# Expert gathers of a two-layer kernel: head 0 of tile 0 chosen alone, V rows eight behind U rows, query steps in thirds

## What is computed

```python
def peer(xn, w_pq, sub_k1, sub_k2, expert_u, expert_v):
    B, S, D = xn.shape
    q = (xn @ w_pq).reshape(B, S, PEER_HEADS, 2, PEER_HALF)
    s1 = jnp.einsum('bshd,hnd->bshn', q[..., 0, :], sub_k1, preferred_element_type=jnp.float32)
    s2 = jnp.einsum('bshd,hnd->bshn', q[..., 1, :], sub_k2, preferred_element_type=jnp.float32)
    v1, i1 = lax.top_k(s1, PEER_TOPK)
    v2, i2 = lax.top_k(s2, PEER_TOPK)
    cand = (v1[..., :, None] + v2[..., None, :]).reshape(B, S, PEER_HEADS, PEER_TOPK * PEER_TOPK)
    vs, ci = lax.top_k(cand, PEER_TOPK)
    e1 = jnp.take_along_axis(i1, ci // PEER_TOPK, axis=-1)
    e2 = jnp.take_along_axis(i2, ci % PEER_TOPK, axis=-1)
    eidx = e1 * PEER_NKEYS + e2
    gates = jax.nn.softmax(vs, axis=-1).astype(xn.dtype)
...
    def block(args):
        xb, ib, gb = args
        act = jax.nn.gelu(jnp.einsum('tkd,td->tk', expert_u[ib], xb))
        return jnp.einsum('tk,tkd->td', act * gb, expert_v[ib])
```

## Time and profile before

| | us |
|---|---|
| median of three runs | 2485.25 |
| profiled execution | 2483.89 |
| its span | 2482.5 |
| PE busy in the span | 2106.7 (85%) |
| VectorE busy | 1411.8 (57%) |
| ScalarE busy | 644.2 (26%) |
| POOL busy | 682.2 (27%) |
| bytes moved by DMA | 751.22 MB, 303 GB/s on average |

### The profile page before, as it was taken

One profiled execution on the slowest core, in us unless ns is written; L12 is line 12 of the kernel. 1 busy time (PEld: TensorE's weight loads), 2 busy tenths in 40 slices (PEclk: granted clock), 3 DMA queues, 4 the chain that ended last, 5 costly groups with the idle time before them and its releaser, 6 DMA issues.

```text
span 2482.5 us, 19393 instructions
## 1 busy us (share of the span) xinstructions
PE 2106.7 (85%) x7532; PEld 1345.7 (54%) x7532; DVE 1411.8 (57%) x1786; ACT 644.2 (26%) x884; POOL 682.2 (27%) x522
## 2 busy tenths in 40 slices
PE   8998948698887787777777777779999999999999
PEld 7876845254432332222222222226888778888887
DVE  4576686645568777454444444445554665654454
ACT  5454522111112010100000000004443353543342
POOL 0000045445455555444454545430000000000000
PEclk9999978999999999999999999989999999999999
DMA  7443469899999999999999999994455544455553
GB/s 274 157 153 104 168 272 398 358 421 397 372 422 421 421 421 422 421 422 421 421 422 422 421 422 422 422 404 160 183 189 194 177 161 170 170 191 195 191 179 143
DMA packets 105355, 751.22 MB, mean 303 GB/s; under 512 B 11952, under 2 KB 11952, under 8 KB 14384
## 3 DMA queue, kind: packets, MB, share of 16 engines
q0 software_dynamic: 73728, 536.90, 52.3%
q1 hardware_dynamic: 29376, 207.63, 23.4%
q10 hardware_dynamic: 2160, 5.45, 0.6%
HBM read 747.84 MB, written 2.10 MB: 302 GB/s over the span
## 4 chain that ended last, share of the span: by engine, by line
PE 51%; DMA 35%; DVE 9%; issue 2%; ACT 1%; POOL 1%; ACTq 0%; SPq 0%; DVEq 0%; POOLq 0%
PE ps L336 37%; DMA xT_rows<-in_expert_v,idx 23%; PE ps L647 10%; DMA wlo_row<-in_expert_v,idx 4%; DMA W<-in_expert_u,idx 2%; DMA xT_rows<-in_expert_u,idx 2%; DMA W<-in_expert_v,idx 2%; DVE wlo L1254 1%; DMA raw<-in_expert_u,idx 1%; DVE raw L1635 1%; PE ps L357 1%; DVE W L1635 1%; PE ps L545 1%; DVE xT_rows L1635 1%; ACT whi L818 1%
## 5 line engine op out<-in xcount | busy, mean ns | idle before, releaser
L336 PE MATMUL ps<-whi,xT 128*128 128x512 f32 x2736 | 664.8, 396 | 14.3 <-ACT whi L818 11.5
L1254 DVE TENSOR_TENSOR wlo<-raw,whi 128x2048 fp32r<-128x2048 f32 x195 | 445.4, 2288 | 282.5 <-ACT whi L818 282.3
L336 PEld LDWEIGHTS ps<-whi,xT 128*128 128x128 f32 x2736 | 515.4, 190 | 130.2 <-issue 15.0
L818 ACT ACTIVATE whi<-raw 128x2048 fp32r<-128x2048 f32 x195 | 372.2, 1914 | 474.4 <-PE ps L336 371.5
L647 PE MATMUL ps<-xT_rows,W 128*128 128x512 f32 x808 | 379.1, 612 | 126.4 <-DMA xT_rows<-in_expert_v,idx 121.5
L336 PE MATMUL ps<-wlo,xT 128*128 128x512 f32 x1368 | 341.0, 392 | 32.5 <-DVE wlo L1254 32.5
L647 PEld LDWEIGHTS ps<-xT_rows,W 128*128 128x128 f32 x808 | 147.8, 193 | 355.0 <-issue 263.8
L1635 DVE CUSTOM_DVE_ANT_0 xT_rows<-xT_rows,W 128x2048 f32<-128x2048 f32 x96 | 219.9, 2291 | 206.2 <-DMA xT_rows<-in_expert_u,idx 205.8
L647 PE MATMUL ps<-W 128*128 128x512 f32 x536 | 255.9, 621 | 90.6 <-DMA W<-in_expert_v,idx 66.2
L336 PEld LDWEIGHTS ps<-wlo,xT 128*128 128x128 f32 x1368 | 257.7, 189 | 88.0 <-DVE wlo L1254 34.5
L647 PE MATMUL ps<-raw,W 128*128 128x512 f32 x512 | 236.1, 604 | 61.7 <-DMA raw<-in_expert_v,idx 56.8
(11 more groups left out here) (275 smaller groups left out, 1469.6 us busy)
## 6 DMA issues: line engine op xcount, KB each, us to landing
raw<-in_weights SPq DMA_DIRECT2D x196, 1024.0 KB, 4.9
h<-in_x SPq DMA_DIRECT2D x8, 256.0 KB, 6.3
out<-h ACTq DMA_DIRECT2D x8, 256.0 KB, 2.8
xT_rows<-in_expert_v,idx POOLq DMA_INDIRECT x106, 15.8
xT_rows<-in_expert_u,idx POOLq DMA_INDIRECT x96, 16.4
W<-in_expert_u,idx POOLq DMA_INDIRECT x70, 16.4
raw<-in_expert_u,idx POOLq DMA_INDIRECT x70, 16.4
W<-in_expert_v,idx POOLq DMA_INDIRECT x70, 15.5
```

Source lines behind the costliest of these rows:

```text
L336: return pe.matmul(ps[:, (banks_of(b) if bank is None else bank) + t, 0:cols_n], x[:, q0 + qn * 4 + k, s], w_[:, cs], start=start, stop=stop)
L818: a.activation(split_into(c)[0], raw[:, RAW_OF[c], :], ACT.Copy).then_inc(sem["hi_done"], 1)
L1254: v.tensor_tensor(lo, raw[:, RAW_OF[c], :], hi.bitcast(F32), ALU.subtract).then_inc(sem["lo_done"], 1)
```

## The change

Head 0 of tile 0 is carried ahead of the rest, in two rounds of eight experts; the V rows follow eight behind the U rows, and gelu and weights are made for eight rows at a time; query steps 6 to 15 are cut into thirds, each behind one V row; heads 2 and 3 are chosen singly. `xn` loses the row scale, which goes into the gelu's scale; tile 1's `xn` is made by POOL. The key chunk is split two chunks earlier, and the FFN gain is loaded earlier. The slots of the last sixteen rows go on in turn. The diff, cut to its core:

```diff
-LAG = 1
+ROWS_OF_TILE = 128
+PICKS = 2 * ROWS_OF_TILE
+LAG = 8
-TAIL = UNITS - LAG
+TAIL = PICKS - LAG
+ROW_ORDER = [("u", i) for i in range(LAG)] + [(kind, i + d) for i in range(PICKS) for kind, d in (("u", LAG), ("v", 0)) if i + d < PICKS]
-FEW_ROWS = ROW_AT["u", 4, 0]
+FEW_ROWS = ROW_AT["u", 68]
+QUERY_AT = {6: 3, 7: 6, 8: 18, 9: 22, 10: 26, 11: 30, 12: 41, 13: 46, 14: 51, 15: 56}
+TURN_AT = {1: 9, 2: 34, 3: 60}
+GATES = [(0, 0, 16), (0, 16, 32), (0, 32, 48), (0, 48, 64), (0, 64, 96), (0, 96, 128), (1, 0, 128)]
+GATES_OUT_AT = {5: 0, 18: 1, 34: 2, 50: 3, 66: 4, 98: 5, 130: 6}
+    "head": [0, 1, 0, 1, 0, 1, 0, 1, 0, 1, 0, 1, 0],
+    "pair": [1, 0, 1, 0, 1, 0, 1, 0, 1, 0, 1, 0, 1],
...
+    last = n - (len(ROW_ORDER) - LAST_ROWS)
+    if last >= 0:
+        return (4, 5, 6, 7, 0, 1)[last % 6]
+    return (n - FEW_ROWS + 4) % GR
...
+            g.wait_ge(*evac_of(B_OUT + 3))
+            g.wait_ge(sem["load_ffn"], 16)
+            g.tensor_tensor(xn[:, 1, :], h[:, 1, :], ffn_row, ALU.mult).then_inc(sem["xn_ok"], 1)
+
             g.wait_ge(sem["lo_done"], C_PQ + 2)
...
                 if n == 4:
-                    g.wait_ge(sem["used"], C_PQ + 4)
+                    g.wait_ge(sem["used"], C_PQ + 3)
...
+                elif kind == "u" and i in (0, 8, 16, 32, 48, 64, 96):
+                    g.wait_ge(sem["chosen"], (0, 8, 16, 32, 48, 64, 96).index(i) + 1)
```

PE, the start (`half_hi` and `half_lo` are the two parts of the old `half_step` for one tile and some slices) and the row loop:

```diff
-            half_step(0, 0, {3: last_entry})
+            half_hi(0, 0, 0, range(4))
+            last_entry()
+            half_hi(0, 0, 0, range(4, 8))
+            half_lo(0, 0, 0, range(8))
             entry_ready(E_FFN, 2)
-            half_step(0, 1, {4: lambda: entry_ready(E_FFN, 3)})
-            half_step(1, 0, {3: lambda: head_turn(0), 6: lambda: head_scores(0)})
-            half_step(1, 1, {})
+            half_hi(0, 1, 0, range(4))
+            half_lo(0, 1, 0, range(4))
+            entry_ready(E_FFN, 3)
+            half_hi(0, 1, 0, range(4, 8))
+            half_lo(0, 1, 0, range(4, 8)).then_inc(sem["first_mm"], 1)
+            half_hi(0, 0, 1, range(2))
+            head_turn(0)
+            half_hi(0, 0, 1, range(2, 8)).then_inc(sem["hi_used"], 1)
+            head_scores(0)
+            half_lo(0, 0, 1, range(8)).then_inc(sem["used"], 1)
+            half_step(0, 1, (1,))
+            half_step(1, 0, (0, 1))
+            half_step(1, 1, (0, 1))
             head_turn(1)
             head_scores(1)
+            tile_turn()
             query_step(4)
+            tile_scores()
             query_step(5)
...
+                for step, at in QUERY_AT.items():
+                    if at <= i < at + 3:
+                        query_part(step, i - at)
+                for block_n, at in TURN_AT.items():
+                    if i == at:
+                        query_turn(block_n)
+                    if i == at + 2:
+                        query_scores(block_n)
```

VectorE, and in the same way ScalarE, in the order of the splits, and VectorE's new row loop:

```diff
             for n in range(4):
                 split(34 + 2 * n)
+                if n == 3:
+                    split(C_KEYS)
                 if n:
                     entry(E_FFN, n - 1)
-                split(35 + 2 * n)
+                split(35 + 2 * n if n < 3 else C_PQ)
                 residual_in(B_OUT + n, C_OUT + 9 + 2 * n, slice(n * NC, (n + 1) * NC))
-            split(42)
-            split(43)
+            split(C_PQ + 1)
...
-            split(45)
+            v.wait_ge(sem["load_ffn"], 16)
+            own(v.tensor_tensor(xn[:, 0, :], h[:, 0, :], ffn_row, ALU.mult))
...
+            def row_step():
+                dot(i)
+                if i and i % LAG == 0:
+                    row_weights(i - LAG)
+                if i in GATES_OUT_AT:
+                    gates_out(GATES_OUT_AT[i])
+                if i == 1:
+                    turned_in(1)
+                    query_step(4)
+                if i == 3:
+                    turned_in(2)
+                if i == 7:
+                    query_step(5)
+                for step, at in QUERY_AT.items():
+                    if i == at + LAG + 1:
+                        query_step(step)
+                for block_n, at in TURN_AT.items():
+                    if i == at + LAG + 2:
+                        query_turn(block_n)
...
+            first_experts(slice(0, 8), 0)
+            query_step(2)
+            first_experts(slice(8, 16), 1)
+            own(v.tensor_copy(gate[:, 0, 0:16], one_head.top[:, 0, :]))
+            query_step(3)
+            gates_in(0)
+            rows_until(6)
+            choose_head(1, by_schedule("head"))
+            rows_until(22)
+            choose_head(2, by_schedule("head"))
+            rows_until(34)
+            choose_head(3, by_schedule("head"))
+            v.wait_ge(sem["xn_ok"], 1)
+            rows_until(47)
+            choose_pair(2, by_schedule("pair"))
+            rows_until(74)
+            choose_pair(3, by_schedule("pair"))
+            rows_until(PICKS)
```

More of the change, by code:

```diff
@@ new lines, in head_scores, with tile_turn, tile_scores @@
+                m.then_inc(sem["query_mm"], 1)
+            def tile_turn():
+                pe.wait_ge(sem["query_lo"], 2)
+                for k in range(4):
+                    m = pe.transpose(ps[:, 2, k * 128:(k + 1) * 128], qb[:, 1, k * 128:(k + 1) * 128], ident[:, :])
+                m.then_inc(sem["query_T"], 1)
+            def tile_scores():
+                pe.wait_ge(sem["query_lo"], 3)
+                pe.wait_ge(sem["query_out"], 2)
+                for k in range(4):
+                    c = slice(k * 128, (k + 1) * 128)
+                    m = matmul3(ps[:, 3, c], (qh[:, k, 128:256], ql[:, k, 128:256]), (KH[:, c], KL[:, c]), start=True, stop=True)
+                m.then_inc(sem["query_mm"], 1)
@@ L586, in query_step, with query_part @@
             def query_step(i):
                 block_step(B_PQ + i // 4, C_PQ + i, i % 4, 4, bank=0)
+            def query_part(i, part):
+                c, b, qn = C_PQ + i, B_PQ + i // 4, i % 4
+                if qn == 0 and part == 0:
+                    pe.wait_ge(evac_of(b - 1)[0], evac_of(b - 1)[1])
+                hi, lo = whi[:, BUF_OF[c], :], wlo[:, BUF_OF[c], :]
+                if part < 2:
+                    pe.wait_ge(sem["hi_done"], c + 1)
+                    for k in (2 * part, 2 * part + 1):
+                        for t in range(NT):
+                            s, cs = slice(t * 128, (t + 1) * 128), slice(k * NC, (k + 1) * NC)
+                            pe.matmul(ps[:, t, :], xh[:, qn * 4 + k, s], hi[:, cs], start=(qn == 0 and k == 0), stop=False)
+                            m = pe.matmul(ps[:, t, :], xl[:, qn * 4 + k, s], hi[:, cs], start=False, stop=False)
+                    if part:
+                        m.then_inc(sem["hi_used"], 1)
+                else:
+                    pe.wait_ge(sem["lo_done"], c + 1)
+                    for k in range(4):
+                        for t in range(NT):
+                            s, cs = slice(t * 128, (t + 1) * 128), slice(k * NC, (k + 1) * NC)
+                            m = pe.matmul(ps[:, t, :], xh[:, qn * 4 + k, s], lo[:, cs], start=False, stop=(qn == 3 and k == 3))
+                    m.then_inc(sem["used"], 1)
@@ new lines, in tensor_program @@
+                pe.wait_ge(sem["diag_ok"], i + 1)
+                row_landed(pe, n)
+                for b in banks:
+                    last = ROWS_OF_TILE - 1 if t == 0 else PICKS - 1 if b < 2 else TAIL - 1
+                    m = pe.matmul(ps[:, (4 if t == 0 else 0) + b, :], diag[:, i % DIAGS, :], slots[SLOT_OF[n]][:, b * NC:(b + 1) * NC],
+                                  start=(i % ROWS_OF_TILE == 0), stop=(i == last))
+                m.then_inc(sem["v_used"], 1)
+                for step, at in QUERY_AT.items():
+                    if at <= i < at + 3:
+                        query_part(step, i - at)
@@ L1639, in peer_in @@
                 v.tensor_tensor(h[:, t, cs], ps[:, bank + b, :], h[:, t, cs], ALU.add).then_inc(sem["peer_in"], 1)
-            def pair_cols(n):
-                return slice(32 * n, 32 * n + 32)
             def nothing():
                 pass
-            def at_step(what, unit, row, chunk):
-                todo, rows_, chunks = iter(SCHEDULE[what]), iter(range(row, 16)), iter(range(chunk, chunk + 4))
-                def go():
-                    for do in next(todo):
-                        if do == "d":
-                            query_step(next(chunks))
-                        else:
-                            dot(unit, next(rows_))
-                return go
@@ new lines, in rows_until, with by_schedule, go @@
+            def rows_until(i):
+                while next_row[0] < i:
+                    row_step()
+            def by_schedule(what):
+                todo = iter(SCHEDULE[what])
+                def go():
+                    for _ in range(next(todo)):
+                        row_step()
+                return go
+            turned_in(0)
+            v.wait_ge(sem["query_out"], 1)
```

(2 more changed lines are left out.)

482 lines of the change are left out of this document (221 added, 261 removed), and 4 rows, old and new, of the table SCHEDULE.

## The result

The changed kernel takes 2465.66 us, the median of four runs (2461.73 to 2467.55), against 2484.79 (2483.07 to 2485.45) for the kernel before beside it: ratio 0.992, 95% interval 0.9905 to 0.9935. A second comparison, with six runs, gave 2467.16 (2460.45 to 2471.33) against 2486.09, ratio 0.9925 (0.9913 to 0.9937). It is faster by 19 us in both comparisons, where 24 were forecast; the time lies in the range. The profiled execution took 2464.38 us, its span 2462.8.

What follows compares the result with a forecast made beforehand. The gather phase was taken as bound by its transfers at 422 GB/s, plus their pauses and its start. Terms summed to -24.2 us from 2483.89, giving 2459.7; with the median 1.36 above, 2461, range 2451 to 2473.

Steps and rivals of the forecast that it cites:

- Start: Up to the first gather: issued 9.8 us earlier, near 322.5, less 1.0 for POOL's multiplication of tile 1 delaying VectorE.
- Rival C: The start doesn't come forward: POOL's multiplication takes over 17 us or holds VectorE; +10, 2471 us; chance 0.08.
- Two more chunks: Query chunks 4 and 5, which landed before the gather phase, now go through within it: +5.0 us.
- 370 to 380: Transfers around the first V row: the 2.4 us lost at 370 to 380 becomes 1.5, so -0.9.
- rival A: First rows starve the queue: V row 0 slips from 361 to 370, transfers pause about 8 us; 2469; chance 0.2.
- Turns and thirds: Turns of query blocks 1 and 2, query steps in thirds: losses of 2.7 and 3.6 us fall to 1.5 each, -3.3.
- Heads 2 and 3: Before U row 32: choosing these heads singly has indices ready in time, removing the 9.3 us transfer loss.
- Eight slots: First eight-slot gather, at 660 to 680: index wait goes, last query step is next; 2.0 of 7.3 us stay, -5.3.
- Tail: Last rows, 1620 to 1687.7: eight V rows left and slots in turn leave 5.0 of 6.6 us lost, -1.6.
- V eight behind U: Groups of eight V rows: twice as many gelus, weights and waits cost nothing while PE waits for transfers; 0 us.
- Rival D: Group boundary: every V group waits for its diagonal, 32 times instead of 16; slower, 2512 to 2553 us; chance 0.06.
- The index waits (B): VectorE's choosing takes more rows than scheduled, so the 9.3 or the 5.3 us returns; 2467 to 2471; chance 0.12.

Runs made afterwards that it cites:

- xn on VectorE: Against the changed kernel, tile 1's xn multiplication is made by VectorE behind the split of query chunk 3, not by POOL; 2462.6 us, ratio 0.9905.
- whole steps: Against the changed kernel, query steps 6 to 15 are whole again, all three thirds behind one V row; 2463.41 us, ratio 0.9915.
- POOL later: Against the changed kernel, POOL's multiplication also waits for the mean and so starts one step later; one run, 2459.82 us.
- pair at 22: Against the changed kernel, heads 2 and 3 of tile 0 are chosen as a pair again, from U row 22 over six rows; 2465.9 us, ratio 0.9923.
- pair at 24: Against the changed kernel, heads 2 and 3 are chosen as a pair, from U row 24 over eight rows; 2474.83 us, ratio 0.9951.
- extra matmuls: Against the changed kernel, PE runs 52 more matmuls into an unread bank while waiting before V row 0; 2464.92 us, ratio 0.9906.
- late chunks: Against the changed kernel, SyncE loads chunk 62 and those behind it only when V row 248 is used; 2463.42 us, ratio 0.9914.

## Why the prediction was right, and where it was short

**Start: -9.8 + 1.0 said, -3.8 measured.** The step that failed is the term for POOL's multiplication, bounded at 0 to 4 and taken as +1.0 "since VectorE has a split to do first in any case". It cost 5.2. The split didn't serve as cover: POOL waited for its end and then ran for 4.61 us, and what VectorE had next was a tiny operation with the transposed slices behind it. Of the 5.2, 4.17 are VectorE's hold (4.34 less 0.17); the rest falls to PE, whose granted clock was 0.72 at 314 to 320, behind 3.76 us of idling, and 1.00 at 308 to 320 with xn on VectorE. Without that multiplication F-A is 18.54, where the steps gave 322.5 - 304.81 = 17.7. So the count of matmuls, transposes and the shorter round were right within a us. Rival C had the mechanism, with a hold of 10; half of that came.

The rule of the Trainium skill ("SBUF — State Buffer", Who interferes with whom) was the better guide. It excludes the other engine for the whole instruction, counts `tensor_scalar` among what can meet GpSimd, and exempts a VectorE instruction with at most one SBUF input outside the two-port modes. The rows above agree: the `tensor_scalar` of two elements ended with POOL's instruction, and the operation on PSUM at 306.31 wasn't held. The prediction took only the case of two SBUF inputs from it. The figure of the Trainium skill for such an operation ("GPSIMD Engine Reference", Performance versus the Vector engine), 4.5 us, agrees with 4.61. What I made of it, a push of 1.8, was short for two reasons: I had the split end, and POOL start, at 307.5 instead of 308.3, and I took the first thing held to be VectorE's multiplication at 310, where it was the small operation at 308.44.

**Two more chunks, +5.0.** Nothing landed from 310 to 328 in the changed kernel, as said. SyncE's loads between F and L, before and after, show the two chunks:

```profile
raw<-in_weights SPq DMA_DIRECT2D x18, 1024.0 KB, 9.2
raw<-in_weights SPq DMA_DIRECT2D x20, 1024.0 KB, 9.1
```

All queues together moved 556.50 MB in that stretch before and 558.61 after, 2.1 MB more, which is 5.0 us at 422 GB/s. (The prediction's "some 19" chunks before were 18.)

**370 to 380, -0.9.** The loss went altogether in this profile (421 GB/s), -2.4. V row 0 came at 370.83, ten later than the 361 said (six of it the late start), and 42.4 behind F instead of 38.5. The reserve of rows was just enough: that is rival A's mechanism, and it bit wherever V row 0 was slow, for 2 to 3 us and not 8. That the changed kernel's own profiles were spared is luck: the clock had just come back.

**Turns and thirds, -3.3.** The losses at both turns are gone here, -6.3. The thirds aren't the cause: whole steps show no more. 1.5 to 1.8 us came back in the 20 us from about 425 in four other profiles (POOL later, pair at 22, pair at 24, extra matmuls). In all four the clock granted there was 0.91, in the changed kernel 1.00. The same V row, in the changed kernel and with the pair at 22:

```profile
435.39 3.70 PE L709 MATMUL ps<-raw,W 128*128 128x512 f32 x8 [0.98 <-ACT W L1144]
433.28 5.26 PE L709 MATMUL ps<-raw,W 128*128 128x512 f32 x8 [0.97 <-ACT W L1144]
```

The kernel before had a lowered clock at the turn of block 2 as well, 0.95 at 565 to 600. So part of the gain is chance, and which edit removed the rest is open.

**Heads 2 and 3, -9.3.** The size was right: in the changed kernel the place alone is worth 9.5 us of transfers and 10.9 of L-F. The name was wrong, for it isn't "singly" that does it. A pair at U row 22 does as well.

**Eight slots, -5.3.** The index wait went and the last query step was next, as named; but the 11.11 us on POOL cost 4.6, not 2.0: the rows and the chunk still under way covered less than counted, and the transfers fell to 325 GB/s at 680 to 700. Of the 7.3 us lost before, 2.7 were gained and not 5.3.

**Tail, -1.6.** 6.8 against 6.6: nothing gained. The rest is what the last V rows on six slots cost; the one try at it didn't test it.

**V eight behind U: 0.** From 1082 on PE waits 1.56 to 1.58 us for the diagonal at a group's start, at every eighth row now, and 700 to 1620 runs at 422, although single waits while tile 1 is chosen are longer (3.32 us before 758.59, 5.45 before 966.39). Rival D never came near. The index waits (B) stayed away, and came back with four rows of delay in the pair at 24, so the margin is under 20 us.

Within the phase errors offset each other: 4.4 us less than said in slots and tail, 4.5 more at 370 and the turns. The sum for L-F hit (15.8 against 15.4) partly by that. Nothing made up for the 5.0 at the start. Not undone alone were the V lag, the order of the last slots, the key chunk's earlier split, the row scale in the gelu and the earlier load of the FFN gain.

## To carry over

When an operation is moved to an idle engine, ask which memory it shares with the busy one. Two-input work on POOL and on VectorE took turns here, so moving 2.3 us from VectorE cost 5.2 on the chain; list what VectorE has to do while POOL runs, down to the smallest operation. Where an in-order queue waits for results of a choice, count the rows between the choice's end and the first use before redesigning it: the place of one choice, four rows at its end, was worth 9.5 us, as much as half of the whole gain. And before valuing a stage's start, look at what else can hold its end: of 5.2 us won there 2.9 arrived, and a pause of 2.4 took the rest.

## What was not expected of the hardware

**A two-element operation held for 4.2 us.** Even 128x2 waits for POOL's whole multiplication. The gather's issue is in it too: 2.29 us at 328.41, beside VectorE's split, against 0.94.

**The granted clock differs at the same place of the same program, and the time with it.** Behind the last V row all kernels run the same program (but for the held loads of the late chunks), and yet that part took 794.8 to 798.7 us. The windows at the attention of the second layer, for the changed kernel and the one with extra matmuls, and PE's rows in them:

```profile
1971.00:1983.00 12.00, 10.42 (x61) 9.06 (x62) 7.20 (x11) 6.19 (x5) 0.00 (x0) 1.00 0.46 171
```

```profile
1971.00:1983.00 12.00, 10.71 (x46) 9.24 (x47) 5.49 (x7) 4.01 (x4) 0.00 (x0) 0.72 0.35 132
```

```profile
1971.80 1.97 PE L367 MATMUL ps<-ident,W 128*128 128x128 f32 x16 [2.15 <-DVE W L1918]
1974.54 1.13 PE L767 MATMUL ps<-W 128*128 128x128 f32 x8 [0.78 <-ACT W L1228]
```

```profile
1971.52 3.04 PE L367 MATMUL ps<-ident,W 128*128 128x128 f32 x16 [2.15 <-DVE W L1923]
1975.34 2.05 PE L772 MATMUL ps<-W 128*128 128x128 f32 x8 [0.78 <-ACT W L1233]
```

The same work after the same wait of 2.15 us takes 1.97 us in one execution and 3.04 in the other. In the eight profiles with the clock at 1.00 from 303 to 312 us behind L, the rest took 794.77 to 794.93; in two with 0.81 there, 796.43 and 796.44; in three with 0.62, 797.60 to 797.70; the late chunks had 0.68 and 798.65, about 1 of which are their own. That the executions of one kernel differ in this way shows in the changed kernel's second comparison. Its six times, with the mean granted clock of each, were 2460.45 (0.987), 2463.29 (0.985), 2465.27 (0.983), 2469.05 (0.981), 2469.28 (0.980) and 2471.33 (0.982). By the stages of the profiles, A lay anywhere from 301.78 to 306.38, V row 0 decided over up to 3.0 us and this last part over 2.9. My estimate is that these three make up most of the 3 to 11 us by which runs of one kernel differ, which is more than most single edits here are worth; the executions without a profile can't show it. Stages between two events inside the program told the edits apart where medians didn't.

What lowers the clock is open. The chip may have a part in it: behind the last V row it was lowered in six of the eight profiles taken on one chip and in none of the four known to be from another. All three kernels with extra matmuls had the 0.62, 1600 us behind those matmuls, so the program may have one too.
